# Up projection by seven products: two pairs of products in turn into two banks, the seventh ahead of the sixth

## The reference

```python
x = layer_norm(DEEPNORM_ALPHA * x + merged @ w_out, ln1_g, ln1_b)
hdn = jnp.square(jax.nn.relu(x @ w_up))                # 1024 -> 4096: the up projection
x = layer_norm(DEEPNORM_ALPHA * x + hdn @ w_down, ln2_g, ln2_b)
```

## Time and profile before

| | |
|---|---|
| median of 3 runs | 2127.92 us (2127.86 to 2128.04) |
| profiled execution | 2128.49 us, its span 2126.5 us |
| TensorE busy | 2112.1 us, 99% of the span |
| VectorE, ScalarE, GpSimd busy | 1045.1, 524.8, 1315.3 us |
| chain that ended last | TensorE 97%, VectorE 3% |
| up projections by seven products | six stretches of 44.7 us |

### The profile page before, as it was taken

The page is one execution under the profiler, slowest core; times in us unless marked ns, Lnnn a source line. Parts: engine busy times, 40 slices in busy tenths (PEclk is TensorE's granted clock), DMA queues, the critical chain, the costliest instruction groups (busy, mean ns, idle before and its releaser), DMA issues.

```text
span 2126.5 us, 38102 instructions
## 1 busy us (share of the span) xinstructions
PE 2112.1 (99%) x15732; PEld 2047.6 (96%) x15732; DVE 1045.1 (49%) x1664; ACT 524.8 (25%) x936; POOL 1315.3 (62%) x1555
## 2 busy tenths in 40 slices
PE   9999999999999999999999999999999999999997
PEld 9898999999999999999998989999999999999997
DVE  6156300534278873626781571006324787726257
ACT  4121021041014141414241210210410141514133
POOL 6844558645683947466757346676457748475575
PEclk9999999999999999999999999999999999999999
DMA  5415424234231223222323153332352313222321
GB/s 177 135 51 171 127 82 138 76 107 162 94 100 60 100 80 100 80 84 79 97 72 119 60 167 111 119 120 72 111 176 80 100 56 103 82 80 80 100 94 52
DMA packets 200325, 215.41 MB, mean 101 GB/s; under 512 B 5601, under 2 KB 192993, under 8 KB 200161
## 3 DMA queue, kind: packets, MB, share of 16 engines
q1 hardware_dynamic: 170688, 172.84, 25.4%
q10 hardware_dynamic: 29472, 40.20, 5.6%
HBM read 199.06 MB, written 13.97 MB: 100 GB/s over the span
## 4 chain that ended last, share of the span: by engine, by line
PE 97%; DVE 3%; ACT 0%; issue 0%; ACTq 0%; DVEq 0%
PE gp L585 53%; PE gp L1113 13%; PE gp L608 9%; PE gp L599 7%; PE qb L688 7%; PE gp L765 3%; PE qb L765 2%; PE gp L955 1%; PE gp L943 1%; PE qb L728 1%; DVE r L2166 1%; DVE x_lo L2072 0%; PE qb L735 0%; DVE m_lo L1673 0%; DVE r L2063 0%; DVE r L2066 0%
## 5 line engine op out<-in xcount | busy, mean ns | idle before, releaser
L467 POOL TENSOR_TENSOR w_lo<-stage,w_hi 128x256 fp32r<-128x256 f32 x1008 | 816.4, 841 | 91.5 <-ACT w_hi L1207 71.5
L464 POOL TENSOR_SCALAR w_hi<-stage 128x1024 fp32r<-128x1024 f32 x240 | 252.3, 1051 | 497.1 <-PE gp L585 245.0
L585 PE MATMUL gp<-b_hi,w_hi 128*128 128x288 f32 x1408 | 321.5, 295 | 0.0
L585 PE MATMUL gp<-x_hi,w_hi 128*128 128x288 f32 x1408 | 321.2, 295 | 0.0
L585 PE MATMUL gp<-b_hi,w_lo 128*128 128x288 f32 x1408 | 318.4, 293 | 0.0
L585 PE MATMUL gp<-b_lo,w_hi 128*128 128x288 f32 x1408 | 318.4, 293 | 0.0
L585 PE MATMUL gp<-x_lo,w_hi 128*128 128x288 f32 x1408 | 318.2, 293 | 0.0
L585 PE MATMUL gp<-x_hi,w_lo 128*128 128x288 f32 x1408 | 318.2, 293 | 0.0
L585 PEld LDWEIGHTS gp<-b_hi,w_hi 128*128 128x128 f32 x1408 | 231.6, 188 | 2.4 <-issue 2.2
L585 PEld LDWEIGHTS gp<-x_hi,w_hi 128*128 128x128 f32 x1408 | 231.4, 188 | 2.3 <-issue 2.1
L585 PEld LDWEIGHTS gp<-b_lo,w_hi 128*128 128x128 f32 x1408 | 231.5, 188 | 1.0 <-issue 1.0
(11 more groups left out here) (303 smaller groups left out, 4272.8 us busy)
## 6 DMA issues: line engine op xcount, KB each, us to landing
stage<-in_w_in SPq DMA_DIRECT2D x54, 1024.0 KB, 5.4
stage<-in_w_up SPq DMA_DIRECT2D x32, 1024.0 KB, 5.3
stage<-in_w_down SPq DMA_DIRECT2D x32, 1024.0 KB, 5.1
stage<-in_w_in SPq DMA_DIRECT2D x40, 256.0 KB, 4.2
stage<-in_w_ret_out SPq DMA_DIRECT2D x8, 1024.0 KB, 5.1
stage<-in_w_mem_kv SPq DMA_DIRECT2D x8, 1024.0 KB, 5.0
stage<-in_w_out SPq DMA_DIRECT2D x8, 1024.0 KB, 5.0
s_in_c<-in_ret_state ACTq DMA_DIRECT2D x8, 512.0 KB, 5.0
```

The source lines that it names most:

```text
L464: nc.gpsimd.tensor_scalar(hi, raw, 1.0, 1.0, ALU.mult, ALU.mult).then_inc(hi_done, 1)
L467: ins = nc.gpsimd.tensor_tensor(lo[:, k:k + 2, :], raw[:, k:k + 2, :], hi[:, k:k + 2, :].bitcast(F32), ALU.subtract)
L585: last = mm(gp[:, 2 * (i % 2) + half, 0:HALF], w[:, i % 4, k * P:(k + 1) * P], x(k, half), start=(k == n == 0), stop=(k == nk - 1 and n == 2))
```

## The change

The order of the seven products is now a table. The first pair of group 1 keeps the order 0 to 6 (`IN_TURN`). The other pairs issue 0 and 2 together, one matmul of each in turn, then 1, then 3 and 4 together in the same way, then 6, then 5 (`BY_TWO`); the last pair of a group issues 0 and 2 together, then 1, 3, 4, 5, 6 (`ENDING`). `nth` gives a product's place in this order, which the waits on `prod_done` now use; `ready` (left out below) holds the waits ahead of each product, which are as before. In the diff the functions stand in the order GpSimd, TensorE, ScalarE, VectorE. The orders of ScalarE and VectorE are changed to match, and GpSimd's wait ahead of the down projection's tiles counts by the new order.

```diff
+IN_TURN = ((0,), (1,), (2,), (3,), (4,), (5,), (6,))
+BY_TWO = ((0, 2), (1,), (3, 4), (6,), (5,))
+ENDING = ((0, 2), (1,), (3,), (4,), (5,), (6,))
...
+    def steps_of(g, p):
+        return IN_TURN if (g, p) == (1, 0) else ENDING if p == 3 else BY_TWO
+
+    def nth(g, p, n):
+        return sum(steps_of(g, p), ()).index(n) + 1
...
     def seven_free(eng, l, g, p, n):
...
-            eng.wait_ge(prod_done, 7 * pair_no(l, g, p - 1) + n + 1)
+            eng.wait_ge(prod_done, 7 * pair_no(l, g, p - 1) + nth(g, p - 1, n))
...
         def split_four(l, first, rows=(KT, KT), high_made=False, behind=None):
...
-                    pool.wait_ge(prod_done, 7 * behind[1] + min(2 * s + 2, 7))
+                    pool.wait_ge(prod_done, 7 * behind[1] + max(nth(behind[0], 3, n) for n in range(2 * s, min(2 * s + 2, 7))))
...
             def seven_products(g, p):
...
-                def one(n, bank, rows, start):
-                    hi, lo = rows
+                factors = {0: (a, rows_of(0, 0), True), 1: (b, rows_of(1, 0), True), 2: (c, rows_sum(0), True),
+                           3: (a, rows_sum(1), False), 4: (c, rows_sum(3), False), 5: (a, rows_sum(2), False),
+                           6: (b, rows_of(1, 1), True)}
+
+                def together(*products):
                     for k in range(4):
-                        for m, (w, x) in enumerate(((w_hi, hi), (w_hi, lo), (w_lo, hi))):
-                            last = mm(gp[:, bank, 0:HALF], seven_slot(w, n)[:, k, :], x[k], start=(start and k == m == 0),
-                                      stop=(k == 3 and m == 2), **({} if start else {"skip_group_check": True}))
-                    last.then_inc(prod_done, 1)
+                        for m in range(3):
+                            for n in products:
+                                bank, (hi, lo), start = factors[n]
+                                w, x = ((w_hi, hi), (w_hi, lo), (w_lo, hi))[m]
+                                ins = mm(gp[:, bank, 0:HALF], seven_slot(w, n)[:, k, :], x[k], start=(start and k == m == 0),
+                                         stop=(k == 3 and m == 2), **({} if start else {"skip_group_check": True}))
+                                if k == 3 and m == 2:
+                                    ins.then_inc(prod_done, 1)
...
+                for products in steps_of(g, p):
+                    for n in products:
+                        ready(n)
+                    together(*products)
                 pe.sem_inc(tile_done, 2)
...
             def seven_high(g, p, n):
...
-                    act.wait_ge(t_made, 4 * q + i)
+                    act.wait_ge(t_made, 4 * q + (4 if i == 2 else i))
...
                     if more:
                         raw_to_bank(g, p + 1)
-                    keep_part(q, 0, a, 0)
+                    keep_part(g, p, 0, a, 0)
+                    keep_part(g, p, 2, 1, 1)
+                    if p:
+                        hidden_high(g, p - 1, 1)
                     if more:
+                        seven_high(g, p + 1, 2)
                         seven_high(g, p + 1, 0)
                     if p:
                         hidden_high(g, p - 1, 0)
                     if more:
                         seven_high(g, p + 1, 1)
-                    keep_part(q, 2, 1, 1)
-                    if more:
-                        seven_high(g, p + 1, 2)
-                    keep_part(q, 3, a, 2)
+                    keep_part(g, p, 3, a, 2)
                     if more:
                         seven_high(g, p + 1, 3)
                         seven_high(g, p + 1, 4)
-                    keep_part(q, 5, a, 3)
+                    keep_part(g, p, 5, a, 3)
                     if more:
                         seven_high(g, p + 1, 5)
-                    hidden_high(g, p, 1)
-                    if more:
                         seven_high(g, p + 1, 6)
+                hidden_high(g, 3, 1)
                 hidden_high(g, 3, 0)
...
             def quarter_out(g, p, which):
...
-                dve.wait_ge(prod_done, 7 * q + n)
+                dve.wait_ge(prod_done, 7 * q + nth(g, p, n))
...
                         weight_sum(g, p + 1, 2)
                         weight_sum(g, p + 1, 3)
-                        sum_low(g, p + 1, 2)
                         weight_sum(g, p + 1, 4)
                     quarter_out(g, p, 1)
+                    if more:
+                        sum_low(g, p + 1, 2)
                     quarter_out(g, p, 2)
-                    squared(p, 1)
                     if more:
+                        quarter_out(g, p, 3)
                         sum_low(g, p + 1, 3)
-                    quarter_out(g, p, 3)
+                        squared(p, 1)
+                    else:
+                        squared(p, 1)
+                        quarter_out(g, p, 3)
                     squared(p, 0)
                     if more:
                         sum_low(g, p + 1, 4)
```

More of the change, by code:

```diff
@@ L1117, in seven_products @@
[L1117 to L1133, removed]
-                pe.wait_ge(part_in, 4 * q + 3)
-                one(5, a, rows_sum(2), False)
-                pe.wait_ge(t_split, 4 * q + 4)
-                pe.wait_ge(quarter_made, 4 * q + 1)
@@ L1138, in seven_products @@
-                one(6, b, rows_of(1, 1), True)
+                        for m in range(3):
[6 more added lines that the diff above has]
+                                    ins.then_inc(prod_done, 1)
@@ new lines, in ready @@
+                def ready(n):
+                    if n == 0:
+                        pe.wait_ge(raw_split, 3 * q + 1)
+                        pe.wait_ge(pair_free[0], l * (TILES // 2) + half_t + 1)
+                    elif n == 1:
+                        pe.wait_ge(raw_split, 3 * q + 2)
+                        pe.wait_ge(pair_free[1], l * (TILES // 2) + half_t + 1)
+                    elif n == 2:
+                        if g == 1 and p == 0:
+                            pe.wait_ge(s_split, l * 4 + 4)
+                        pe.wait_ge(t_split, 4 * q + 1)
+                    elif n == 3:
+                        pe.wait_ge(t_split, 4 * q + 2)
+                        pe.wait_ge(part_in, 4 * q + 1)
+                    elif n == 4:
+                        pe.wait_ge(raw_split, 3 * q + 3)
+                        pe.wait_ge(part_in, 4 * q + 2)
+                    elif n == 5:
+                        pe.wait_ge(t_split, 4 * q + 3)
+                        pe.wait_ge(part_in, 4 * q + 3)
+                    else:
+                        pe.wait_ge(t_split, 4 * q + 4)
+                        pe.wait_ge(quarter_made, 4 * q + 1)
@@ L1607, in seven_high, with keep_part @@
                 else:
-                    act.wait_ge(t_made, 4 * q + i)
+                    act.wait_ge(t_made, 4 * q + (4 if i == 2 else i))
                     act_fn(seven_slot(w_hi, n), t_sum((0, 1, 2, 3)[i - 1]), ACT.Copy).then_inc(t_high, 1)
-            def keep_part(q, n, bank, i):
-                act.wait_ge(prod_done, 7 * q + n + 1)
+            def keep_part(g, p, n, bank, i):
+                q = pair_no(l, g, p)
+                act.wait_ge(prod_done, 7 * q + nth(g, p, n))
                 if q:
@@ L1633, in _ @@
                 for p in range(4):
-                    q, a, more = pair_no(l, g, p), (0, 3)[p % 2], p < 3
+                    a, more = (0, 3)[p % 2], p < 3
                     if more:
                         raw_to_bank(g, p + 1)
-                    keep_part(q, 0, a, 0)
+                    keep_part(g, p, 0, a, 0)
+                    keep_part(g, p, 2, 1, 1)
+                    if p:
+                        hidden_high(g, p - 1, 1)
                     if more:
+                        seven_high(g, p + 1, 2)
                         seven_high(g, p + 1, 0)
@@ L2222, in quarter_out @@
                 t, a = relu_of(p), (0, 3)[p % 2]
-                n, parts, i, bank, column, half = ((2, 1, 0, 2, 0, 0), (5, 3, 2, 1, 1, 0),
-                                                   (6, 4, 1, a, 1, 1), (7, 4, 3, 2, 0, 1))[which]
+                n, parts, i, bank, column, half = ((1, 1, 0, 2, 0, 0), (4, 3, 2, 1, 1, 0),
+                                                   (5, 4, 1, a, 1, 1), (6, 4, 3, 2, 0, 1))[which]
                 if which == 0:
                     dve.wait_ge(hid_ready, l * 32 + g * 8 + max(2 * p - 2, 0) + 2)
-                dve.wait_ge(prod_done, 7 * q + n)
+                dve.wait_ge(prod_done, 7 * q + nth(g, p, n))
                 dve.wait_ge(part_in, 4 * q + parts)
@@ L2289, in _ @@
                             weight_sum(g + 1, 0, 3)
+                            weight_sum(g + 1, 0, 4)
                             sum_low(g + 1, 0, 2)
-                            weight_sum(g + 1, 0, 4)
                         elif m == 6:
```

1 line of the change is left out of this document (added).

## The result

The changed kernel took 2132.71 us (median of 13 runs, 2131.99 to 2133.22) beside 2128.07 us for the kernel before (13 runs, 2127.86 to 2128.66): a ratio of 1.0021, 95% interval 1.0012 to 1.0029, so 4.6 us slower. The forecast was 2125.9 us, its range 2124.8 to 2130.8. The profiled execution took 2131.99 us, its span 2130.2, which is 3.7 longer than before's 2126.5.

The account below looks back on a forecast made before the run. TensorE bounds the kernel: in the up projection, number of matmuls by their spacing at full clock. Terms -2.2 - 0.4 + 0.6 = -2.0 us take the profiled 2128.49 to 2126.5, the median to 2125.9; range 2124.8 to 2130.8.

Parts of the forecast that it names:

- Spacing: Up projection's 22 and 16 blocks in turn: 130.0 ns a matmul, 2.2 us gained; at 133.3 ns, 0.9 us lost.
- The second product's wait: Up projection pairs except a group's first: second product, now starting later, loses its 0.02 us wait; 0.4 us gained.
- The queues behind a pair's start: ScalarE, VectorE and GpSimd work in the middle pairs: every slack 0.7 us or more, so costed at nothing.
- The third rival: The 16 blocks of fourth and fifth product wait for ScalarE's copies: 6.4 us slower, 2132.3 us; chance 0.09.
- The end of a group: GpSimd starts later on the down projection's first tile: 0.1 us in each of six groups, 0.6 us lost, 0 to 2.4.
- no gain from the turns: Blocks in turn stay at the down projection's first tile's 133 ns: 2129.0 us; chance 0.37.
- More than 130: Two products with separate weights and banks overlap further, at 126 ns: 3.6 us more gained, 2122.3 us; chance 0.04.

## Why the prediction was wrong, step by step

**Spacing, -2.2 us: wrong.** The blocks took 3.19 us, not 3.12. The step that failed is the choice between the ends: I took 130.0 because most rows of line 585's turns have it, and kept the down projection's first tile as the far end. The first tile came out as the nearer row (132.9 there, 132.8 to 132.9 in the blocks), but my reason for keeping it, that it follows a product, does not tell it apart: the third tile of the same rows follows 24 matmuls into one bank (the second tile goes `by_half`) and runs at 130.0. The price of this end was also off: 133.3 ns on every block gave 0.9 us lost. The third product's 1.58 us in rows 5 belonged to the wait ahead of it; in the new order whole it takes 1.60, so first and third stand at 3.18 and the block loses 0.01, not 0.04. All six stretches together: -0.22 us.

**The second product's wait, -0.4 us: right in kind, not in size.** The wait is gone, and the second product has lost its 0.02 us: 1.58 us in the run of whole products, with no distance of starts over 135 ns. But the six stretches gain 0.15 us by it, not 0.4. The term counted the second product alone. Behind the wait the third product had taken 1.58 to 1.60 us and the fourth mostly 1.596; without it both take 1.60, which gives back more than half: a pair takes 11.160 us, and took 11.168 in the mean of the 18.

**The queues behind a pair's start, 0: right.** I laid the two copies of first and third from 3.3 to 4.0 us into the pair, and the block that overwrites their banks at 4.7. ScalarE in the pair that starts at 885.74:

```profile
888.99 0.71 ACT L1638 ACTIVATE part<-gp 128x288 f32<-128x288 f32 x2
```

That is 3.25 to 3.96, and the block starts 0.80 us later, at 890.50. No wait on line 1128 exists. The third rival, slower by the copies, gave 2132.3 us, almost the measured time, by a mechanism that did not occur: a time that fits shows no cause.

**The end of a group, +0.6 us with 0 to 2.4: the step that sank the forecast.** It measured +3.78 at the first tiles and +0.89 behind group 3. Three parts of it failed.

First, which instruction lies beside which. I let GpSimd's 1.05 us pass fall on the second square and stretch it to 1.17. My own layout had the two hidden lows running to 908.9 on the clock of before, over the first square's start at 907.85, and I did not lay the two engines side by side. Done with the numbers of that paragraph and with the 0.6 us by which the square outlasts the pass in rows 9 and 10: first square until 908.9 + 0.6 = 909.5, not 909.02; GpSimd's pass, held until then, until 909.5 + 1.05 = 910.55; the second square until 911.15, not 910.28; the lows 0.87 us later than before, with 0.33 us of slack. That is 0.54 us late in each of six groups, 3.2 us, worked out from rows that were there. The measured delay is 0.80 us and 0.49 late.

The Trainium skill, "SBUF — State Buffer", section "Who interferes with whom", says that a VectorE instruction with two inputs in SBUF contends with a GpSimd instruction that reads SBUF, that the port pair they share is an exclusive lock, and that issue order decides who blocks. The runs agree: the squares, with both inputs in SBUF, wait for the rest of GpSimd's instruction (0.76, 1.17, 1.72 us), and GpSimd's pass waits for the square (1.56 us, not 1.05), while a lowered sum, one of whose inputs is in PSUM, keeps its 0.69 us beside GpSimd (18 such in the kernel before). I had not weighed it against this part.

Second, the charge for a slack that is nearly used up. I took 0.1 us a group, by analogy with the second product, which is ready 0.27 us early and pays 0.02. A lateness of 0.49 us cost 0.60 to 0.64 us a tile, and one of 0.06 us cost 0.35 in the run with the last pair in its old order (408 and 208 ns between starts, not 133). So being late costs the lateness and some 0.1 to 0.3 us more, and an analogy from the early side says nothing of it. My bound of 0.4 us a group was an assumption, with no row behind it.

Third, the layer ends. GpSimd's late start was followed to the second tile only. In group 3 GpSimd goes on through all eight tiles without a pause. Its last lows there, and TensorE:

```profile
1035.58 4.75 POOL L476 TENSOR_TENSOR w_lo<-stage,w_hi 128x256 fp32r<-128x256 f32 x4
```

```profile
1039.93 0.29 PE L617 MATMUL gp<-b_hi,w_lo 128*128 128x288 f32 x1
1040.38 0.40 PE L617 MATMUL gp<-b_hi,w_hi 128*128 128x288 f32 x1 [0.17 <-POOL w_lo L476]
```

They end at 1040.33, 0.27 us behind the time (1040.06) at which TensorE is due. In the kernel before they ended 35.5 us after the down projection's start and now 36.8, so the first tile's stall of 0.64 us hides half of the 1.3. The two layers lose 0.43 and 0.37 us here, which is 0.80 of the +0.89; of the rest 0.08 us lies in the last layer's third tile, for a reason that I did not find. I did not ask which of GpSimd's tiles is needed with the least to spare.

**The rivals.** The first, no gain from the turns, is what happened in the up projection. With both parts as measured it gives 2128.07 - 0.22 + 3.78 + 0.89 = 2132.5 against 2132.71. It needed both that rival and a group's end outside its bounds to leave my range. More than 130 did not occur: no 24 matmuls of this width in the stretches read took less than 3.115 us, 129.8 ns each. The 122.5 ns that the prediction took from the Trainium skill, "TensorE: Matmul & The Clock Gate", section "Back-to-back issue gap", did not occur either; that section gives the formula for an isolated matmul and says that in a stream the weight loads help to set the spacing, which the prediction left out.

## What to carry to other kernels

When a wait's place moves, move on paper everything that the waiting engine does afterwards, and lay it beside the other engines' rows at their times, not beside their durations; where an engine's instruction has different durations at different places, find out what lies beside it first. A slack of 0.3 us on one engine can be used up by another that is 62% busy and on no critical chain. Where TensorE does not wait, an order of matmuls is worth at most its spacing; here the best arrangement tried, which also stored the sums elsewhere, took 0.17 us off 44.66.

## What the runs showed of the hardware that was not expected

VectorE's square of 128 x 576 (two SBUF inputs, 0.76 us when free) ends 0.59 to 0.62 us after the GpSimd instruction during which it was issued, wherever that stretches it: so in the kernel before (the first square), the changed one (both squares), the one with only the late start (both), and, with 909.43 and 910.03, the one with the last pair in its old order, and alike in all six groups. Its duration is therefore set by how much of that instruction is left, up to 1.75 us here.

Matmuls of 288 columns at full clock start 130.0, 131.7 or 133.3 ns apart, all without a wait. A product alone has 131.7 where every row of its right factor begins at a multiple of 2304 bytes from the start of `x` or of the sums, and 133.3 where some or all begin 1152 bytes beyond; moving the sums alone changed the one into the other. Turns between two banks with different weights keep 130.0 in a down projection; turns over the two halves of `x` have 130.0 to 130.3 in a pair that follows such turns and 132.9 to 133.3 in the pairs that follow a single product of sums; turns over a half and a sum of `x` have 132.8 to 132.9 with either entry, and 131.5 to 131.7 with the sums stored side by side. What decides among turns is not settled by these runs.
